# Merge kept as rows of channels, its up projections and the last output projection by seven block products

## The reference, cut to what matters

```python
def first_block(x, ...):
    out_a = from_heads(fox_attention(qa, ka, va, log_f)) @ w_fox_up[l]
    out_b = from_heads(nsa_attention(...)) @ w_nsa_up[l]
    mix = jax.nn.sigmoid(g_a) * out_a + jax.nn.sigmoid(g_b) * out_b   # g_a, g_b: columns of h @ w_in
    x = x + mix @ w_out[l]
    x = x + hierarchical_moe(rms_norm(x, norm_ffn_g[l]), ...)
def second_block(x, ...):
    merged = g_a * y_a + g_b * y_b
    h = h + rmsnorm(merged @ w_o, g_post)
```

## Time and profile before

| | |
|---|---|
| time, median of 3 runs | 1475.31 us |
| the profiled execution's own time / its span | 1475.47 us / 1474.2 us |
| PE busy | 1394.8 us, 95% of the span |
| DVE, ACT, POOL busy | 554.3, 351.5, 270.0 us |
| the merge, from its first matmul to `out7`'s first (344.8 to 502.4 us) | 157.6 us, PE busy 155.1 |
| experts (580 to 868 us) | 288.0 us, PE busy 279.9, DMA share 0.98 |
| from the last projection's first matmul to the end (1410 to 1474.2 us) | 64.2 us, PE busy 56.5 |

### The profile page before, as it was taken

How to read it: one execution, slowest core, us unless ns; L and a number is a source line. 1 busy time by engine, 2 the same in 40 slices (tenths; PEclk the granted TensorE clock), 3 DMA queues, 4 the chain that set the end, 5 groups by cost and what they waited for, 6 DMA issues and landing times. The chain is left out here.

```text
span 1474.2 us, 23732 instructions
## 1 busy us (share of the span) xinstructions
PE 1394.8 (95%) x10084; PEld 747.5 (51%) x10084; DVE 554.3 (38%) x1340; ACT 351.5 (24%) x833; POOL 270.0 (18%) x303
## 2 busy tenths in 40 slices
PE   7998999899999997999999989989999899999997
PEld 5545545565444445444444434446777445655543
DVE  3124423573212534421211143335369382343403
ACT  2225324543101111111111133344211201322221
POOL 3010302204040721122222122010241002111000
PEclk9999999999999998999999999989999999999999
DMA  6164013400312248999999961010140331300311
GB/s 203 58 235 143 1 59 86 150 26 4 113 59 93 101 176 289 318 377 375 379 381 379 392 231 72 8 57 7 52 171 29 82 120 38 123 3 17 117 55 58
DMA packets 98973, 207.78 MB, mean 141 GB/s; under 512 B 14533, under 2 KB 22544, under 8 KB 98736
## 3 DMA queue, kind: packets, MB, share of 16 engines
q1 hardware_dynamic: 87152, 171.38, 32.3%
q0 software_dynamic: 11712, 34.83, 7.1%
HBM read 185.73 MB, written 19.42 MB: 139 GB/s over the span
## 5 line engine op out<-in xcount | busy, mean ns | idle before, releaser
L466 PE MATMUL pb<-Wt,HT 128*128 128x512 f32 (+1 forms) x384 | 152.7, 556 | 1.0 <-DMA Wt<-in_w_in_dram 1.0
L3617 PE MATMUL pb<-Wt,HT 128*128 128x512 f32 x256 | 119.4, 608 | 2.1 <-DVE AR L3708 2.1
L466 PE MATMUL pb<-Wt,AR 128*128 128x512 f32 x256 | 111.5, 592 | 0.0
L466 PEld LDWEIGHTS pb<-Wt,HT 128*128 128x128 f32 x384 | 70.6, 205 | 70.2 <-issue 70.1
L2054 PE MATMUL pb<-AR 128*64 128x512 f32 x256 | 85.0, 595 | 0.7 <-issue 0.7
L678 PE MATMUL pb<-AR 64*128 64x512 f32 (+7 forms) x256 | 65.3, 500 | 14.1 <-ACT AR L773 4.4
L466 PEld LDWEIGHTS pb<-Wt,AR 128*128 128x128 f32 x256 | 48.1, 190 | 57.9 <-issue 57.9
L3617 PEld LDWEIGHTS pb<-Wt,HT 128*128 128x128 f32 x256 | 47.0, 192 | 53.7 <-issue 48.9
L2054 PE MATMUL pb<-Wt,AR 128*64 128x512 f32 x192 | 70.8, 595 | 0.0
L777 ACT ACTIVATE AR<-AR,SM 128x512 f32<-128x512 f32 (+3 forms) x96 | 53.1, 554 | 51.6 <-DVE SM L729 51.2
L729 DVE CUSTOM_DVE_ANT_0 AR<-pb,AR 128x512 f32<-128x512 f32 (+3 forms) x96 | 43.2, 487 | 57.7 <-PE pb L680 57.4
(11 more groups left out here) (562 smaller groups left out, 2363.6 us busy)
## 6 DMA issues: line engine op xcount, KB each, us to landing
Wt<-in_w_in_dram SPq DMA_DIRECT2D x18, 2048.0 KB, 8.6
AR<-in_w_gate_dram SPq DMA_DIRECT2D x8, 2048.0 KB, 18.3
AR<-in_w_up_dram SPq DMA_DIRECT2D x8, 2048.0 KB, 18.7
AR<-in_w_down_dram SPq DMA_DIRECT2D x8, 2048.0 KB, 18.4
Wt<-in_w_gate_dram SPq DMA_DIRECT2D x6, 2048.0 KB, 17.5
Wt<-in_w_down_dram SPq DMA_DIRECT2D x6, 2048.0 KB, 14.4
Wt<-in_w_up_dram SPq DMA_DIRECT2D x6, 2048.0 KB, 21.3
ys<-AR POOLq DMA_DIRECT2D x1, 6144.0 KB, 21.9
```

The source lines that it names most:

```text
L466: r = mm(s[:, 0:n], lT[:, k, t * 128:(t + 1) * 128], w[:, k, c0:c0 + n], start=k == 0, stop=k == nk - 1)
L3617: r = mm(s, HT[:, k, t * 128:(t + 1) * 128], W.ap(("gate2", c, br))[:, k, :], start=k == 0, stop=k == 7)
```

## The change

1. The merge is made of eight units of `Quarters`: per branch two for the gates and two for the up projection, which so goes by seven products too. All results are kept as rows of channels (channels on partitions, tokens along the row), the layout that `out7` reads, so the 32 transposes and ACT's copies of them go. The sum over the branches is made by DVE as whole rows (L1741, 128x512, both operands in SBUF), four after each of the last two units. POOL makes weight sums for each unit and token sums for the two branches' features.
2. The last output projection goes by `Seven` (`fin7`): POOL makes its sums, and the final norm of the lower tokens squares the upper half ahead.
3. All four quarter copies of expert 15's last rows are ACT's; DVE makes none for it.

```diff
         def merge_po():
             po.wait_ge(s_loc, 1)
-            for b in range(2):
-                gate7[b].right_po()
-
...
+            for n, u in enumerate(merge7):
+                u.right_po()
+                if n == 0:
+                    left_sums_po(foT, 2, up_sums, s_uleft[0])
+                if n == 4:
+                    po.wait_ge(*P.filled(merge7[3].key("y")))
+                    left_sums_po(noT, 2, up_sums, s_uleft[1])
 
...
+            for n, u in enumerate(merge7):
+                if n == 2:
+                    pe.wait_ge(s_loc, 1)
+                u.p1_pe()
+                if n:
+                    merge7[n - 1].p4_pe()
+                u.p5_pe()
+                u.p2_pe()
+                u.p6_pe()
+                u.p3_pe()
+                u.p7_pe()
+            u.p4_pe()
...
+                for c in range(2):
+                    g, u = merge7[4 * b + c], merge7[4 * b + 2 + c]
+                    u.p5_ve()
+                    ve.wait_ge(*P.drained(g.key("x")))
+                    ve.wait_ge(*P.filled(u.key("x")))
+                    vt.tensor_tensor(u.c11, u.view("x"), u.c11, ALU.mult).then_inc(P.free(u.key("x")), 1)
+                    u.p6_ve()
+                    ve.wait_ge(s_sg, 3 * (2 * b + c + 1))
+                    ve.wait_ge(*u.read(1))
+                    ve.wait_ge(*P.filled(u.key("z")))
+                    vt.tensor_tensor(copies[2], u.view("z"), copies[2], ALU.add).then_inc(P.free(u.key("z")), 1)
+                    ve.wait_ge(*P.drained(u.key("z")))
+                    ve.chain(lambda: vt.tensor_tensor(u.c12, u.c12, copies[2], ALU.mult))
+                    ve.wait_ge(*u.read(0))
+                    ve.wait_ge(*u.part(3))
+                    vt.tensor_tensor(copies[1], u.view("y"), copies[1], ALU.add).then_inc(s_read4, 1)
+                    ve.wait_ge(*u.read(2))
+                    ve.chain(lambda: vt.tensor_tensor(u.c22, u.c22, copies[1], ALU.mult))
+                    ve.wait_ge(*P.filled(u.key("y")))
+                    vt.tensor_tensor(up_last, u.view("y"), copies[0], ALU.add).then_inc(P.free(u.key("y")), 1)
+                    ve.wait_ge(*P.drained(u.key("y")))
+                    ve.wait_ge(*P.drained(u.key("x")))
+                    ve.chain(lambda: vt.tensor_tensor(u.c21, u.c21, up_last, ALU.mult))
+                    ve.after()
                     if b:
-                        ve.wait_ge(*P.drained(key))
-                        ve.wait_ge(*P.drained(("mu", 0, (t, c))))
-                        vt.tensor_tensor(m, m, s, ALU.add).then_inc(s_mix, 1)
+                        for m in range(4 * c, 4 * c + 4):
+                            vt.tensor_tensor(mixT[:, m, :], mix[:, m, :], to[:, m, :], ALU.add).then_inc(s_mix, 1)
...
         def ffn_norm_po():
             out7.right_po()
-            for x in uitems:
-                po.wait_ge(*P.drained(("mt", x)))
+            po.wait_ge(s_mix, 8)
             out7.left_po(mixT)
```

The experts' row copies:

```diff
             def down(b):
                 ve.wait_ge(*P.filled(("yb", b)))
-                if b >= LATE:
+                if b == 15:
+                    return
+                if b == LATE:
                     for i in range(2):
                         ve.wait_ge(s_yst[i], 32 * 3 * (LATE // 2))
                     for i in range(2):
                         if i:
-                            ve.wait_ge(s_ycopy, b - LATE + 1)
+                            ve.wait_ge(s_ycopy, 1)
                         r = vt.tensor_copy(*last_quarter(b, i))
                     r.then_inc(P.free(("yb", b)), 1)
                     return
@@ -2214,9 +2364,9 @@
...
+                    for i in range(0 if b == 15 else 2, 4):
                         r = st.copy(*last_quarter(b, i))
-                    r.then_inc(s_ycopy, 1)
+                    r.then_inc(P.free(("yb", b)) if b == 15 else s_ycopy, 1)
                     return
                 if b > 1:
```

And the end of the program:

```diff
         def last_pe():
-            for c in range(2):
...
-                        for d in range(2):
-                            mixed_turn_pe(d, 3)
+            def ready(c, i):
+                pe.wait_ge(*P.drained(("mxt", c, i)))
+
+            w = fin7.steps_pe(mxT, ready)
+            next(w)
+            for d in range(2):
+                mixed_turn_pe(d, 3)
+            for _ in w:
+                pass
...
+            for i in range(2):
+                end(i, 1, P.drained(fin7.key("z", i)))
+            for i in range(2):
+                q = slice(2 + i, 3 + i)
+                ac.wait_ge(*fin7.read(2, i))
+                st.activation(junk[2 + i], yo[:, 2 + i, 512:1024], ACT.Square, accum_out=fss[:, q]).then_inc(s_half, 1)
+            for i in range(2):
+                ac.wait_ge(s_half, 2)
+                end(2 + i, 0, P.drained(fin7.key("y", i)))
+
...
+            def root(t):
                 q = slice(t, t + 1)
-                ve.wait_ge(*P.drained(("wo2", 0, t)))
                 ve.wait_ge(*square_h.nxt())
                 ve.chain(lambda: vt.tensor_tensor(fss[:, q], fss[:, q], fst[:, q], ALU.add))
                 ve.after()
                 rstd_ve(frs[:, q], fss[:, q], 1024, fm[:, q], fy[:, q])
...
+            def first_rows(i):
+                ve.wait_ge(*P.drained(fin7.key("x", i)))
...
-                ve.wait_ge(*P.drained(("wo2", 1, t)))
-                vt.tensor_tensor(yo[:, t, :], yo[:, t, :], X[:, t, :], ALU.add).then_inc(s_yo, 1)
+                vt.tensor_tensor(yo[:, i, :], yo[:, i, :], X[:, i, :], ALU.add).then_inc(s_yo, 1)
+
+            def with_third(i):
...
+                ve.wait_ge(*fin7.read(0, i))
+                vt.tensor_tensor(high[2 + i], y[i], high[2 + i], ALU.add).then_inc(s_sum7, 1)
+
+            def high_gain(i):
+                ve.wait_ge(s_half, i + 1)
+                ve.chain(lambda: vt.tensor_tensor(high[2 + i], high[2 + i], gp[1], ALU.mult))
+
+            def with_last(i):
+                key = fin7.key("y", i)
+                ve.wait_ge(*P.filled(key))
+                vt.tensor_tensor(low[2 + i], y[i], fin7.p1[i], ALU.add).then_inc(P.free(key), 1)
+                ve.wait_ge(*P.drained(key))
+                ve.chain(lambda: vt.tensor_tensor(low_g[i], low[2 + i], gp[0], ALU.mult))
+
+            def last_rows(i):
+                t = 2 + i
+                root(t)
+                for c, s in enumerate((low_g[i], high[t])):
+                    r = vt.scalar_tensor_tensor(out=yo[:, t, 512 * c:512 * c + 512], in0=s, scalar=frs[:, t:t + 1],
+                                                in1=xt(t, c), op0=ALU.mult, op1=ALU.add)
+                    if c:
+                        r.then_inc(s_yo, 1)
+                    else:
+                        ve.count(r)
...
+            first_rows(0)
+            with_third(0)
+            first_rows(1)
+            with_third(1)
+            high_gain(0)
+            high_gain(1)
+            with_last(0)
+            last_rows(0)
+            with_last(1)
+            last_rows(1)
...
         def last_po():
             po.wait_ge(*P.filled(("akrk", 3, 1)))
...
             gt.dma_start(X[:, :, :], xv).then_inc(s_fin, 16)
+            po.wait_ge(s_out2, 4)
+            po.wait_ge(*P.filled(("oAt", 3)))
+            fin7.right_po()
+            for c in range(2):
+                po.wait_ge(*P.drained(("g2", 0, c, 3)))
+                for t in ALLT:
+                    po.wait_ge(*P.drained(("mxt", c, t)))
+            fin7.left_po(mxT)
```

More of the change, by code:

```diff
@@ L311, in build @@
         s_sum7 = sem("product_sums_ready")
+        s_mleft = sem("merge_token_sums_ready")
+        s_uleft = [sem(f"branch{b}_sums_ready") for b in range(2)]
+        s_right4 = sem("weight_sums_ready")
+        s_part4 = sem("block_sum_products_ready")
+        s_first4 = sem("first_block_products_copied")
+        s_read4 = sem("block_sums_read")
         s_sg = sem("merge_gates_ready")
@@ L1483, in build @@
+        mix = Place(AR, ARN, base1).take(8, 512)
+        sg1 = Place(AR, ARN, 8192).take(8, 512)
         mixT = HT
@@ L1496, in build @@
-        uitems = [(t, c) for t in ALLT for c in range(2)]
-        def gate_ready(b, t, c):
-            if t < 2 and c == 0:
-                return P.drained(gate7[b].key("x", t))
-            return s_sg, 6 * b + {(0, 1): 1, (1, 1): 2, (2, 1): 3, (3, 1): 4, (2, 0): 5, (3, 0): 6}[(t, c)]
+        copies = [ar.take(2, 256) for _ in range(3)]
+        ar = Place(AR, ARN, 25600)
+        quarter_sems = s_part4, s_first4, s_read4, s_right4
+        rights = [ar.take(4, 256) for _ in range(3)]
+        gate_use = dict(sems=(*quarter_sems, s_mleft), tokens=HT, weights=lambda tag: (tag, W.ap(tag)),
+                        lefts=(left_sums[0], left_sums[1], HT[:, 0:4, 256:512], left_sums[2]),
+                        rights=rights, copies=copies, late=None)
@@ new lines, in build @@
+        up_sums = [Place(AR, ARN, x).take(2, 256) for x in (21504, 18432, 18944)]
+        up_last = Place(AR, ARN, 20992).take(2, 256)
```

(10 more changed lines are left out.)

412 lines of the change are left out of this document (195 added, 217 removed).

## The result

The changed kernel is slower: 1491.62 us, median of 4 runs (1482.42 to 1497.40), against 1474.91 of the kernel before in the same comparison; the ratio is 1.0096, 95% interval 1.0064 to 1.0129. The same kernel ran three times more, each time on another chip: 1.0087 (1.0056 to 1.0119, 4 runs), 1.0045 (1.0020 to 1.0070, 12 runs) and 1.0049 (1.0029 to 1.0070, 12 runs). The forecast was 1480.5, a ratio of 1.0034. The direction was right. The first result lies 11 us above the forecast and outside its range; of the repeats the first is as far off, and the two longer ones are near it. One run of the kernel before that counts as slow (2861.32 us, one of 27 beside e5 to e8) is left out of the ratios.

A forecast was written before the change was run, and what follows sets the result against it. PE, busy 95% of the span, was taken to bound the kernel. The terms 1475.5 + 11.0 (merge) - 4.0 (experts' end) - 1.8 (last projection) gave 1480.7, median 1480.5 us; range 1464 to 1487.

The forecast's parts named there:

- The hold: Merge's end: each two-SBUF DVE L1741 waits out one POOL sum, 4.9 us each; PE stands 17.5 us.
- the merge: From the merge's first matmul to out7's z products: loses 11.0 us, bounds 9 to 13.
- the first weight sum: Merge's start: PE waits 1.9 us for POOL's first weight sum for the first unit.
- the changes from gates to up projection: Two places in the merge: the copy of the first product comes about 0.55 us late.
- The half clock there: Behind PE's stand at the merge's end: PE restarts at half clock, 3.0 us added.
- The first rival: Merge's row of four L1741: DVE keeps its place, only the first is held; total 1468.5 us, chance 0.25.
- The experts' end: Late expert rows: ACT's copies let PE start sooner and partly keep full clock; -4.0 us, between 2.3 and 5.2.
- PE starts at 866.2: Experts' late rows: PE starts after ACT's four copies end at 866.1, 2.3 us sooner than before.
- The last projection: Last output projection and tail: 8 of 64 matmuls fewer, less new waits; -1.8 us, between -4.6 and 0.
- wait for z: Last projection: PE reaches z ahead of POOL's first token sum and waits 0.6 us more.
- the tail: Kernel's end: from PE's last matmul to DVE's end takes 7.2 us against 4.9 before.
- The clock costs more: Rival: PE's stand and the new start wait bring two more slow stretches; 1488 us, chance 0.12.

The follow-up runs named there:

- e5: The kernel before, unchanged, profiled on the second chip: 1489.66 us.
- e8: The kernel before with the change's last projection and tail alone: ratio 0.9991 to the kernel before, 12 runs.
- e4: The changed kernel with POOL's four weight sums for out7 moved behind the mix, in turns with the token sums: 1485.66 us, ratio 1.0010 to the kernel before.
- e15: The changed kernel with DVE's four L1741 of the second last unit moved behind the last unit's PSUM-reading L1605, L1720 and L1609: ratio 1.0026 to the kernel before.
- e1: The changed kernel again, no edit, on a second chip: 1498.43 us, ratio 1.0087 to the kernel before.
- e13: The changed kernel with 18 filling matmuls in PE's stand ahead of the last unit's third product: ratio 1.0045 to the kernel before, 12 runs.
- e10: The kernel before with the change's merge alone, on the third chip: ratio 1.0056 to the kernel before, 12 runs.
- e9: The changed kernel again, no edit, on the third chip: ratio 1.0045 to the kernel before, 12 runs.
- e12: The changed kernel with POOL's sums for out7 and fin7 reordered by need, fin7's behind DVE's two L3726: 1466.81 us, ratio 0.9900 to the kernel before.
- e14: The changed kernel again, no edit, on the fourth chip: ratio 1.0049 to the kernel before, 12 runs.
- e11: The changed kernel with 36 filling matmuls in PE's stand ahead of the last unit's third product: ratio 1.0094 to the kernel before.

## Why the prediction was right or wrong

**The hold, and the merge: right.** Forecast L1741 at 4.9 us each, a stand of 17.5 at the third product, z products 11.0 later. Measured 4.9, 17.00 and 10.8; the first weight sum cost 1.65 for 1.9, the changes from gates to up projection 0.19 each for 0.55. e4 and e15 show the cause. The half clock there cost 2.6 for the 3.0 counted. The first rival (DVE keeps its place through the row) fell: each of four linked by nothing was held once.

**The experts' end: right in size on the first chip, wrong about the wait.** From the last expert's product to DVE's first addition of late rows the gain was 4.5 us for 4.0, 1.7 of it from the wait and 2.8 from the clock. But "PE starts at 866.2", 1.6 us after the last product, took ACT's copies for the only thing left to wait for. PE stood 2.23, and what ended last was its own branch: at 888.8, 0.4 behind ACT's last copy. On the chips where the branch takes 6.0 to 7.2 us (e1 to e8, e13 to e15), it stands in the place of the wait that was removed, and the kernel before waits there as long (4.90 in e5). On the third chip the kernel with the old copies (e10) waits 2.63 there and the one with the new (e9) 2.24. The clock's part is no steady gain either: in e12 the same wait of 2.23 comes ahead of four records of 3.56 us. The rows that would have told are PE's branch of 3.63 us and the instruction packet at 864.2.

**The last projection: right in sum.** DVE's hold 2.06 for 2.2, no wait for z for 0.6, the tail from PE's last matmul to DVE's end 6.2 for 7.2, against it 1.7 of half clock, which the forecast did not have. From first matmul to DVE's end 59.3 us against 60.9: -1.7 for -1.8. That it agrees so well is luck: the wait for z that did not come, the shorter tail and the slow stretch cancel.

**The time: wrong.** The step that failed is the last one: "1475.5 (own time of the profiled execution) + 11.0 - 4.0 - 1.8", "the median lies 0.2 below that execution", with an own range of 1475 to 1485. No term of the sum is missed by enough: the merge came at 10.8 for 11.0, the experts' end at 4.5 for 4.0, the last projection at 1.7 for 1.8, and the 24 runs of e9 and e14 give 1.0047, which is 1482.4 on 1475.5, 1.9 above the forecast. What failed is the base: the sum stood on one execution, and no term and no width of the range allowed for what executions differ by in code that no edit touches. Three runs within 3 us made it look small. 23 runs of the kernel before on one chip (e9's) span 1473 to 1487, and their time falls by 1.1 us for each 0.001 of mean granted clock. The first four runs after had a mean clock of 0.9675 and e1's four 0.9667; the 24 of e9 and e14 had 0.9708. For the first four that is 3.6 us. The start is the second part: PE's 80 small matmuls began at 28.3 in the profile before, and at 28.1 to 33.1 in the sixteen others, the unchanged kernel's 31.1 among them; 3.4 us in the profile after. In the profiled pair these losses were partly made good by luck, the 5.9 us less half clock behind the experts. The clock's 3.6 and the sum's own miss of 1.9 are 5.5 of the 10.3 us by which the mean of the four, 1490.8, lies above the forecast. A late start like the traced one would be most of the rest, but three of the four runs left no trace, so this stays open.

**"The clock costs more": nearest in time, not shown as a mechanism.** It gave 1488, and the first two series had a lower clock than the forecast counted. Whether the stand brought this is not shown: where filling it was tried (e13), the changed kernel had no more half clock than the kernel before in its first profile (25.8 us against 26.5), so there was little to take away, and nothing was gained.

## What to carry to other kernels

Ahead of moving weight sums to POOL, list DVE's instructions with two SBUF operands that are queued in that time and who waits behind them: each waits out one POOL sum. Place such sums by when they are needed, and the short work that others wait for ahead of the long; here that turned a loss of 0.5% into a gain of 1%. Set a range by how runs of the unchanged kernel differ over many executions, with the clock of each beside it, and not by three of them. And where the busiest engine branches, read the branch's own duration: it can outlast the wait that an edit removes.

## What the runs showed of the hardware that I had not expected

- A branch on PE takes 3.4 to 3.6 us where the DMA share is 0.02 to 0.39 in its first us (the first and the third chip), and 6.0 to 7.2 us where it is 0.97 to 1.06 with weight loads (e1 to e8, e13 to e15), while the same branch takes 0.05 to 0.07 us on DVE, ACT and POOL. The instruction packet inside it comes 1.0 to 1.1 us after the branch's start in the one case and 3.0 to 4.0 in the other.
- With a stand of 17 us filled, a slow stretch was gone there and the next one, at a place with gaps, was longer, for the same cost in the two profiles (2.4 us saved, 2.6 given back).
- X's second quarter reaches ACT at 6.76 us in the first profile before, at 7.85 in e5, the same kernel, and at 8.24 in the first profile after, whose code there is the same. The 80 small matmuls start 2.8 and 3.4 us later in the last two; in e11 they start late too, at 32.6, though the quarter comes at 6.85, so it is not the only cause.
